# A decoder stack on one core: the head of each feed-forward part takes its products in another order

## The reference, cut to what matters

```python
for layer in range(4):
    g = norm_gains[layer]
    h = x + 0.5 * swiglu(rmsnorm_2(x, g[0]), w_ffn_gu[layer, 0], w_ffn_down[layer, 0])
    xn = rmsnorm_2(h, g[1])
    mix = ...                      # hgrn2, mlstm, swa, hgrn2
    h = h + mix
    h = h + 0.5 * swiglu(rmsnorm_2(h, g[2]), w_ffn_gu[layer, 1], w_ffn_down[layer, 1])
    gate = sigmoid(rmsnorm_2(h, g[3]) @ w_ple_gate[layer])
    x = h + gate * (p[layer] @ w_ple_proj[layer])

def swiglu(x, w_gu, w_down):       # x 256 x 1024, w_gu 1024 x 5632, w_down 2816 x 1024
    g, u = split(x @ w_gu, 2, axis=-1)
    return (silu(g) * u) @ w_down
```

## Time and profile before

| | us |
|---|---|
| median of 3 runs | 2399.87 |
| lowest, highest | 2398.66, 2399.9 |
| the profiled execution's own time | 2407.7 |
| its span, first to last instruction | 2405.7 |
| PE busy | 2392.4 (99%) |
| DVE busy | 1727.9 (72%) |
| ACT busy | 1342.0 (56%) |
| granted TensorE clock | 1.00 |

### The profile page before, as it was taken

The page is one execution under the profiler, slowest core; times in us unless marked ns, Lnnn a source line. Parts: engine busy times, 40 slices in busy tenths (PEclk is TensorE's granted clock), DMA queues, the critical chain, the costliest instruction groups (busy, mean ns, idle before and its releaser), DMA issues.

```text
span 2405.7 us, 51567 instructions
## 1 busy us (share of the span) xinstructions
PE 2392.4 (99%) x20328; PEld 2362.4 (98%) x20328; DVE 1727.9 (72%) x2431; ACT 1342.0 (56%) x2044; POOL 78.8 (3%) x77
## 2 busy tenths in 40 slices
PE   9999999999999999999999999999999999999999
PEld 9999999999999999999999999999999999999999
DVE  8879867668776677667766686688667766877666
ACT  5756655447564465445644564467446644766444
POOL 1000000001100000000000000000000000220000
PEclk9999999999999999999999999999999999999999
DMA  7325326555355556555465565644655655535653
GB/s 269 115 64 174 123 80 226 185 184 162 128 187 190 197 170 211 190 184 185 140 202 197 171 210 191 196 137 137 202 188 183 202 195 189 166 124 192 196 196 125
DMA packets 115377, 418.85 MB, mean 174 GB/s; under 512 B 12832, under 2 KB 14112, under 8 KB 114976
## 3 DMA queue, kind: packets, MB, share of 16 engines
q1 hardware_dynamic: 114096, 412.40, 52.3%
q0 software_dynamic: 560, 2.10, 0.3%
q10 hardware_dynamic: 576, 2.27, 0.3%
HBM read 414.62 MB, written 2.10 MB: 173 GB/s over the span
## 4 chain that ended last, share of the span: by engine, by line
PE 94%; DVE 3%; ACT 2%; DMA 1%; issue 1%; POOL 0%; ACTq 0%; SPq 0%; DVEq 0%
PE ps_gu L140 17%; PE ps_gu L146 17%; PE ps_gu L141 17%; PE ps_acc L140 9%; PE ps_acc L146 8%; PE ps_acc L141 8%; PE ps_acc L2744 1%; PE ps_acc L2302 1%; DVE w_lo L100 1%; PE ps_misc L140 1%; PE ps_gu L2338 1%; PE ps_misc L146 1%; PE ps_misc L141 1%; PE ps_sum L140 1%; PE ps_sum L146 1%; PE ps_sum L141 1%
## 5 line engine op out<-in xcount | busy, mean ns | idle before, releaser
L100 DVE TENSOR_TENSOR w_lo<-w_raw,w_hi 128x1024 fp32r<-128x1024 f32 x781 | 953.6, 1227 | 367.3 <-ACT w_hi L92 359.5
L140 PE MATMUL ps_gu<-xn_hi,w_hi 128*128 128x256 f32 x3832 | 1051.6, 279 | 1.2 <-DVE w_lo L100 0.5
L141 PE MATMUL ps_gu<-xn_hi,w_lo 128*128 128x256 f32 x3832 | 1042.7, 276 | 0.0
L92 ACT ACTIVATE w_hi<-w_raw 128x1024 fp32r<-128x1024 f32 x781 | 820.2, 1056 | 368.2 <-PE ps_gu L146 270.3
L146 PE MATMUL ps_gu<-xn_lo,w_hi 128*128 128x256 f32 x3832 | 1001.2, 277 | 0.0
L140 PEld LDWEIGHTS ps_gu<-xn_hi,w_hi 128*128 128x128 f32 x3832 | 719.2, 188 | 4.1 <-issue 2.0
L141 PEld LDWEIGHTS ps_gu<-xn_hi,w_lo 128*128 128x128 f32 x3832 | 719.4, 188 | 0.4
L146 PEld LDWEIGHTS ps_gu<-xn_lo,w_hi 128*128 128x128 f32 x3832 | 692.9, 188 | 0.2
L140 PE MATMUL ps_acc<-h_hi,w_hi 128*128 128x256 f32 x1496 | 415.5, 278 | 0.2 <-DVE h_lo L576 0.2
L146 PE MATMUL ps_acc<-h_lo,w_hi 128*128 128x256 f32 x1496 | 413.6, 276 | 0.0
L141 PE MATMUL ps_acc<-h_hi,w_lo 128*128 128x256 f32 x1496 | 413.5, 276 | 0.0
(11 more groups left out here) (479 smaller groups left out, 2573.4 us busy)
## 6 DMA issues: line engine op xcount, KB each, us to landing
w_raw<-in_w_dram SPq DMA_DIRECT2D x781, 512.0 KB, 4.0
const<-in_const_dram SPq DMA_DIRECT2D x1, 1216.0 KB, 8.5
distance_rows<-arena POOLq DMA_DIRECT2D x1, 1024.0 KB, 7.8
p_all<-distance_rows POOLq DMA_DIRECT2D x2, 512.0 KB, 5.3
p_all<-in_p_dram ACTq DMA_DIRECT2D x1, 1024.0 KB, 6.0
out_dram<-x_res SPq DMA_DIRECT2D x8, 128.0 KB, 1.9
x_res<-in_x_dram ACTq DMA_DIRECT2D x1, 512.0 KB, 6.6
x_res<-in_x_dram SPq DMA_DIRECT2D x1, 512.0 KB, 6.0
```

The costliest lines, as they stand in the source:

```text
L92: act.activation(self.w_hi[:, s, :], self.w_raw[:, r, :], ACT.Copy).then_inc(self.w_hi_ready.sem, 1)
L100: dve.tensor_tensor(self.w_lo[:, s, :], self.w_raw[:, c % NR, :], self.w_hi[:, s, :], ALU.subtract)\
L140: pe.matmul(out, self.w_hi[:, s, j0:j0 + width], rhs_hi, start=start, stop=False, skip_group_check=True)
L141: pe.matmul(out, self.w_lo[:, s, j0:j0 + width], rhs_hi, start=False, stop=False, skip_group_check=True)
```

## The change

The head of a part has a new order on PE: high products 0 to 6 of g and g+1, then high products 0 to 6 of g+2, then high products 7 of all three, then the means, then the eight low products of g+2, and last the sixteen low products of g and g+1. In every down block, PE waits for `h_hi` ahead of the first matmul and for `h_lo` only ahead of the third. On ACT the high part of chunk g+6 is made behind `h_hi` of tile 0 in all heads (before: in C alone). On DVE the low part of g+6 is made behind `h_lo` of tile 0 in all heads, in A that of g+5 too; in A the low parts of g+3 and g+4 leave the fold and come behind `outer` and behind the scaling of tile 0; in C the low part of g+2 leaves the head for the end of `ple`, behind the seventh `xn_lo` and ahead of the fold's first step.

```diff
         def down(t, c, i):
-            pe.wait_ge(*hl.at(b0 + t + 1 + STEP * i))
+            pe.wait_ge(*hh.at(b0 + t + 1 + STEP * i))
             k.wait_chunk(pe, c, i)
             for m in range(KD):
-                mm = k.products(pe, k.ps_acc[:, m // 2, (m % 2) * S:(m % 2 + 1) * S], c % NS, m * P, P,
-                                k.h_hi[:, t % 2, :], k.h_lo[:, t % 2, :], False, t == FT - 1,
-                                start=(t == 0 and m % 2 == 0))
+                out = k.ps_acc[:, m // 2, (m % 2) * S:(m % 2 + 1) * S]
+                k.with_hi(pe, out, c % NS, m * P, P, k.h_hi[:, t % 2, :], t == 0 and m % 2 == 0)
+                if m == 0:
+                    pe.wait_ge(*hl.at(b0 + t + 1 + STEP * i))
+                mm = k.with_lo(pe, out, c % NS, m * P, P, k.h_lo[:, t % 2, :], t == FT - 1)
...
                     if j == KD - 1:
-                        mm.then_inc(k.chunk_done.sem, 1)
+                        mm.then_inc(k.chunk_done.sem, 1 + n)
+            next_out = k.ps_gu[1][:, 0:S]
+
+            def begin_next():
+                pe.wait_ge(*free[1])
+                k.wait_chunk(pe, c0 + 2)
+
+            def next_high(j):
+                k.with_hi(pe, next_out, (c0 + 2) % NS, j * P, P, k.xn_hi[:, j, :], j == 0)
+
             for j in range(KD - 1):
                 high(j)
-            for j in range(KD - 2):
+            begin_next()
+            for j in range(KD - 1):
+                next_high(j)
+            high(KD - 1)
+            next_high(KD - 1)
+            sum_rows(k, pe, k.norms, k.summed)
+            for j in range(KD):
+                pe.wait_ge(*lo_at[j])
+                k.with_lo(pe, next_out, (c0 + 2) % NS, j * P, P, k.xn_lo[:, j, :], False)
+            for j in range(KD):
                 low(j)
-            high(KD - 1)
-            low(KD - 2)
-            low(KD - 1)
-            sum_rows(k, pe, k.norms, k.summed)
...
     def _(act):
...
             k.hi(act, g + AHEAD, i)
-            behind = t == 0 and late[1]
             if t == 0:
                 act.preload_act_table_set("natural_log_exp_and_others")
-            if not behind:
+            else:
                 k.hi(act, g + 1 + AHEAD, i)
...
             act.activation(k.h_hi[:, t % 2, :], k.h[:, t % 2, :], ACT.Copy).then_inc(hh.sem, 1)
-            if behind:
+            if t == 0:
                 k.hi(act, g + 1 + AHEAD, i)
...
     def _(dve):
...
-            if t == 0 and k.inner:
-                k.inner.outer(dve)
-            if not behind:
+            inner = k.inner if t == 0 else None
+            if inner:
+                inner.outer(dve)
+                k.lo(dve, g + 3)
+            elif not behind:
                 k.lo(dve, g + AHEAD, i)
-                if not (t == 0 and k.inner):
+                if t:
                     k.lo(dve, g + 1 + AHEAD, i)
...
-            if t == 0 and k.inner:
-                k.lo(dve, g + 1 + AHEAD, i)
+            if inner:
+                k.lo(dve, g + 4)
...
-            if behind:
+            if behind or inner:
                 k.lo(dve, g + AHEAD, i)
+            if t == 0:
                 k.lo(dve, g + 1 + AHEAD, i)
...
     # ple, on DVE
         if nxt:
             nxt.split_lo(dve, KD - 2)
+            k.lo(dve, to_ffn[0])
             nxt.fold_step(dve, 0)
...
-    k.late = to_ffn[2:], to_ffn
+    k.late = to_ffn[2:], to_ffn[1:]
...
     # OutProjection.finish, on DVE
-            k.lo_for(dve, c0 + KD - 2)
+            if not inner:
+                k.lo_for(dve, c0 + KD - 2)
             fold(dve, 1)
             nxt.split_lo(dve, KD - 1)
             fold(dve, 2)
-            k.lo_for(dve, c0 + KD - 1)
+            if not inner:
+                k.lo_for(dve, c0 + KD - 1)
```

More of the change, by code:

```diff
@@ L494, in tile @@
                 return first()
-            if t == 1:
-                pe.wait_ge(*free[1])
             if t >= 2:
@@ L499, in tile @@
             for n, c in enumerate((at_g(t), at_g(t) + 1)):
+                if t == 1 and n == 0:
+                    continue
                 k.wait_chunk(pe, c, i)
[L501 to L510, removed]
+                for j in range(KD):
+                    mm = k.products(pe, k.ps_gu[t % 2][:, n * S:(n + 1) * S], c % NS, j * P, P,
+                                    k.xn_hi[:, j, :], k.xn_lo[:, j, :], False, j == KD - 1,
+                                    start=(n == 0 and j == 0))
                 mm.then_inc(k.chunk_done.sem, 1)
```

## The result

| | before | changed |
|---|---|---|
| median, us | 2399.9 (5 runs, 2398.66 to 2416.93) | 2452.96 (5 runs, 2442.58 to 2459.7) |
| ratio | | 1.0195 [1.0163, 1.0227] |
| the profiled execution's span, us | 2405.7 | 2440.4 |
| PE busy, us | 2392.4 | 2427.8 |

The changed kernel is slower by 53 us in the medians and 47 in the means, far outside the predicted range. The forecast was "no change". The five runs of before happen to lie low: the same kernel run again beside the experiments had medians of 2401.4 to 2407.4, so the loss is nearer 47 than 53. One of those runs (3489.8 us, granted clock 0.64) is left out of the ratios.

The account below looks back on a forecast made before the run. PE, busy 99% of the span, was taken as the bound. Terms -0.9 + 0.0 + 0.8 + 2.5 + 0.3 - 0.9 - 1.25 + 0.4 = +0.95, taken as +0.7 us, gave 2400.6 on the 2399.87 median; range 2391 to 2411.

Parts of the forecast that it names:

- Heads B, four: Second down block behind heads B: h_lo of tile 1 ready about 711.1, wanted 711.6; cost 0, up to 0.3 a head.
- slow rhythm: Matmuls inside head A's part at 0.1187 us each instead of 0.1132, same clock; 8.2 us of the profiled execution.
- Rival 1: New stalls at second down blocks of C and A lock parts into the slow rhythm, 8.2 us each; chance 0.38.
- Rival 2: Head A's part leaves the slow rhythm, which the earlier timed runs had: 2392.4 us; chance 0.17.
- Head A's means: Both means in head A start without waiting, at 368.08 and 368.51; gain 0.9 us (0 to 1.1).
- Head A's first down block: PE stands 0.26 us for h_hi and 0.23 for h_lo, 0.49 against 0.47 before: no gain.
- Head A's second down block: Four low parts and a later load delay h_lo to near 384.1, wanted at 383.2: 0.8 us lost (0 to 1.3).
- Heads C: PE stands 0.50 us at g+2 and 0.32 at the mean: 0.82 a head, 2.5 us in three.
- C's second down block: h_lo of tile 1 ties with PE's need: 0.1 us a head, 0.3 in three (0 to 0.5 a head).
- Last down blocks: Last down block of seven parts: the 0.13 us stalls go, 0.9 us gained, with no gap left.
- The split waits as a whole: Down blocks: stalls gone -0.9 us, slow rhythm behind four of them gone -1.25, 0.4 back as waits at mixers' heads.
- The rule weighed: The skill's single matmul gap, 109 ns here: a stall would cost only its own length; the trace's two paces disagree.

Follow-up runs that it names:

- number 1: The kernel before with chunk g+2 in threes, its block of sixteen high products removed, nothing else moved: 2445.22 us, ratio 1.0187.
- number 3: The changed kernel with chunk g+3 taking its sixteen high products in pairs ahead of its eight low ones: 2408.65 us, ratio 1.0024.
- number 7: The changed kernel with pairs of high products ahead of low ones in g+3 and every gate chunk from tile 2 on: 2401.41 us.
- number 5: The kernel before with sixteen high products ahead of eight low ones in every tile's gate chunk: 2399.77 us, ratio 0.998.
- number 6: number 5 with the down blocks' split waits for h_hi and h_lo added: 2398.12 us, ratio 0.9975.
- number 10: number 7 with PE's old head order, keeping the DVE and ACT moves and split waits, pairs in every gate chunk: 2400.17 us.
- number 9: number 1 with the mean matmuls issued twice in heads A and B and in ple: 2461.55 us, ratio 1.0235.
- number 2: The changed kernel with PE's old head order; DVE and ACT moves and split waits stay: 2423.75 us, ratio 1.0069.
- number 8: number 6 with pairs ahead of low products also in project, the output projection and ple: 2398.11 us, ratio 0.9973.

## Why the prediction was wrong

**The step that failed** is "Heads B, four", "Cost 0 (up to 0.3 a head)". It looked only at whether an operand is late. None is: PE never stands in these heads, in either kernel. What changed is the order of matmuls behind the means, and the sum had no term for it. The prediction put the new order at nothing there; the runs show 8 to 9 us for each of the four parts. The slow rhythm itself was seen and priced well (8.2 us a part, 8 to 9 measured), but I held stalls for its only start. The trace of before had the evidence against that: behind the means of each head B the spacing is 0.119 for some ten matmuls without a stall, and then it recovers in the block of pairs. I had read only the distance at the means and not the pace behind them, and never asked what ends the rhythm. Rival 1 had the right mechanism of loss with the wrong start: it gave "2417 with two, 2425 with three", while the four parts B were slow in the changed kernel's profile and one to three more are added by its times. The last sentence of the prediction named the sign, "the pace changes in parts whose head has no stall", and it came. Numbers 1, 3 and 7 show the cause from both sides: taking the block away from before gives the loss, giving it back to the changed kernel removes it.

**Rival 1's own places** were right as places. The stall at the third matmul of C's second down block is there, and in the changed kernel and number 3 it locked a part. In the profiled execution it locked one C of three; the third C had a stall of 0.09 us at the first matmul of that block and stayed fast.

**Rival 2**, that head A's part leaves the rhythm, came true in the profiled execution of the changed kernel, but without the gain: by their times, the runs that gave before its median hadn't been slow there.

**The median of before.** "The timed runs may well have been without it" holds for its three timed runs. In 72 further runs of it, taken beside the experiments, 32 lie at 2398 to 2402, 29 about 8 us higher and 11 about 16.

**The other steps**, with the rhythm taken out by numbers 5 to 7, came out nearly as worked out:
- Head A's means: predicted at 368.08 and 368.51, measured at 368.04 and 368.47; `outer` predicted at 369.15, measured 369.10. Right. The stretch from 368.08, where the first mean was due, to the second product behind the means shrank from 2.0 us to 0.9, so the gain is there, and is the 1.1 given for it with the slow first matmul.
- Head A's first down block: predicted stalls of 0.26 and 0.23, 0.49 in all. Measured: four spacings in a row of 0.19, 0.23, 0.23 and 0.22, together 0.42 above the regular spacing, against 0.47 before. Right in sum, the parts spread otherwise.
- Head A's second down block: 0.8 predicted, none in the changed kernel. DVE made the four low parts in one go, 4.62 us (the row at 374.98), and didn't wait for the load of g+8, so `h_lo` ended at 383.17, not 384.1. Mis-sized by 0.8, inside its bounds of 0 to 1.3. With the old head order (number 10) the stall was 0.79.
- Heads C: 0.50 at g+2, measured 0.47 (902.40 to 902.99, less a spacing); 0.32 at the mean, measured 0.23 (905.23 to 905.57, less a spacing) and 0.08 more in front of the second mean row. Right.
- Heads B: `h_lo` of tile 1 was to be 0.5 us early (711.1 against 711.6, two times for which the prediction shows no working). In the first B of the changed kernel it ends at 701.90 and its matmul starts at 703.20, so it is early by 1.3. The wait was right at nothing; the cost lay elsewhere.
- C's second down block: 0.1 predicted; 0.18 in the first C, none in the second, 0.09 in the third. The predicted tie.
- Last down blocks: no spacing above the regular one in any of the eight. Right.
- The split waits as a whole: -0.9 - 1.25 + 0.4 = -1.75 predicted, 1.65 between numbers 5 and 6.
- The moves and the head order as a whole: -0.9 + 0.0 + 0.8 + 2.5 + 0.3 = +2.7 predicted, +3.3 between numbers 6 and 7. Number 10 divides it into 2.0 for the moves and 1.2 for the order.

So +0.7 was a fair sum of the waits (number 7 against number 5: +1.6), and the waits were 3% of what happened.

**The rule weighed** was no way out: the runs show two steady spacings, 0.1133 and 0.1189 us, at a granted clock of 1.00, in every trace of this case. The Trainium skill, TensorE: Matmul & The Clock Gate, section "Back-to-back issue gap", gives one figure for an isolated warm matmul, 109 ns here as an estimate. Of streams of weight loads and matmuls it says that both operations set the spacing, and gives one sustained figure each for 128 and for 512 columns, none for 256. Two steady spacings of one stream are not what it describes, and the traces show them.

**What stays open.** What decides in the heads A and C. In the twelve traces all 48 parts B follow the rule: slow behind the means every time, ended in the block of pairs in all 36 that have one, slow to the end in the 12 that have none (changed, numbers 1 and 9). In A and C the block behind the means failed nine times: in two heads C of number 2, all three of number 10, one of number 6, and in head A of numbers 5, 6 and 8. And parts C left the rhythm without it: all three in number 1, in number 9 and in the changed kernel. A wait of the means doesn't divide them, since the second head C of number 2 had waited as long as the other two and was back at the regular pace within five matmuls, and the one of number 6 had not waited at all. What else differs between the kinds of head was not varied. The means as what starts the rhythm rest on the rows next to them in every trace; a kernel without them was not tried. Which of A and C lock in a given execution changes from run to run, and what in the engine holds the rhythm no run here can show.

## What to carry to other kernels

Where PE is busy 99% of the time, read its pace (length of a window by the count of starts) in every stage, before and behind each irregular instruction, and not only its waits: an order of matmuls that costs nothing in any wait can cost 5% of a stage. When a change moves a block of matmuls, ask what the block did to those behind it; here sixteen high products without low ones between them ended a slow rhythm that had begun at the mean matmuls. Times of one kernel that lie at even steps are a sign of such a state, and small gains are to be measured on a variant in which the steps are gone.

## What the runs showed of the hardware

- At one granted clock (1.00), alternating weight loads and matmuls of 256 columns run at 0.1133 or at 0.1189 us each, steadily, for up to 1593 matmuls.
- The slow rhythm began behind a stall of PE among products in threes (0.18 us was enough in the changed kernel, at 920.63), and behind mean matmuls without any wait, there in all 48 heads B of the twelve traces. The start behind the first product is then held back by 0.19 to 0.31 us where a regular spacing is 0.113.
- A stall doesn't always start it, and four starts in a row held back at 0.19 to 0.23 us ended it (head A of the changed kernel).
- Sixteen high products, w_hi and w_lo in turn on one moving operand, ended it in about twelve matmuls in all 36 heads B that have them (behind the means, or in g+3 in numbers 3 and 7). Behind B, 24 low products and products in threes never did (12 of 12). The last sixteen of those low products are two by two on one moving operand as well (the w_hi of g and of g+1 on the same xn_lo), so behind B sharing the moving operand alone isn't what ends it.
- Behind heads A and C neither holds: the block behind the means failed in nine of them (numbers 2, 5, 6, 8 and 10), and the rhythm ended without it in all three heads C of the changed kernel and of numbers 1 and 9.
- A kernel on one core at clock 1.00 has times some 8 us apart from run to run, and with pairs in each tile the steps are gone: 35 runs of before from 2398.98 to 2417.57, 12 of number 5 from 2398.85 to 2401.34.
